# Two mixers of a hybrid trunk with another order of their TensorE groups, and two thirds of the second router's logits moved ahead

## What is computed

```python
def run_trunk(x, ...):
    for layer in range(2):
        h = rmsnorm(x, norm_mix[layer])
        if layer == 0:
            out = ab_mixer(h, ...)    # 4 heads mLSTM (matrix memory) and 4 heads retention with rotary q, k
        else:
            out = gdn_mixer(h, ...)   # 8 heads gated delta rule after a short convolution
        x = x + out
        x = x + hier_moe(rmsnorm(x, norm_ffn[layer]), ...)   # top group of 4, top 2 of its 8 experts
    return rmsnorm(x, norm_final)

def gdn_step(S, q, k, v, beta, g):   # one chunk; eg = exp(cumsum(g)), gam = decay between positions
    A = tril(beta * (k @ k.T) * gam, -1) + I
    u = solve(A, v * beta);  w = solve(A, k * (beta * eg))
    v_new = u - w @ S
    o = (q * eg) @ S + ((q @ k.T) * gam) @ v_new
    S = exp(g_last) * S + (k * exp(g_last - cumsum(g))).T @ v_new
```

## Time and profile before

| | |
|---|---|
| median of three runs | 1463.34 us (1462.14 to 1463.89) |
| profiled execution | 1466.4 us, of it the span 1464.6 us |
| mean granted TensorE clock | 0.909 |
| TensorE busy | 1153.2 us, 79% of the span |
| VectorE, ScalarE, GpSimd busy | 471.8, 250.5, 65.4 us |
| read from and written to HBM | 449.55 and 3.35 MB, 309 GB/s over the span |
| chain that ended last | PE 51%, DMA 38%, DVE 6%, issue 2% |

### The profile page before, as it was taken

How to read it: one execution, slowest core, us unless ns; L and a number is a source line. 1 busy time by engine, 2 the same in 40 slices (tenths; PEclk the granted TensorE clock), 3 DMA queues, 4 the chain that set the end, 5 groups by cost and what they waited for, 6 DMA issues and landing times.

```text
span 1464.6 us, 27531 instructions
## 1 busy us (share of the span) xinstructions
PE 1153.2 (79%) x11710; PEld 717.3 (49%) x11710; DVE 471.8 (32%) x1211; ACT 250.5 (17%) x633; POOL 65.4 (4%) x100
## 2 busy tenths in 40 slices
PE   8999889878585776775899989888867768767675
PEld 6645546444252443442478666556534434434342
DVE  1023445432232221322343746345222213222133
ACT  2123214110010100100232414131100101010011
POOL 2001102100000000000200101001000000000001
PEclk9999899998998887889899999999998879898888
DMA  9843235999999999999833303139999999999994
GB/s 274 184 92 112 77 122 224 420 411 428 427 429 429 429 428 430 426 429 430 258 120 115 117 4 130 60 118 380 424 428 427 428 428 429 428 430 428 428 428 190
DMA packets 54146, 453.87 MB, mean 310 GB/s; under 512 B 5680, under 2 KB 6480, under 8 KB 29760
## 3 DMA queue, kind: packets, MB, share of 16 engines
q1 hardware_dynamic: 52176, 448.35, 75.8%
q0 software_dynamic: 1904, 4.58, 1.2%
HBM read 449.55 MB, written 3.35 MB: 309 GB/s over the span
## 4 chain that ended last, share of the span: by engine, by line
PE 51%; DMA 38%; DVE 6%; issue 2%; ACT 1%; SPq 1%; POOL 1%; DVEq 0%; ACTq 0%; POOLq 0%
PE bank L341 49%; DMA W<-in_moe_w_up 37%; PE bank L344 1%; DMA W<-in_ab_w_in 1%; SPq L2484 1%; DVE zT L2332 1%; DVE HN L1593 0%; DVE HN L1573 0%; ACT zT L1538 0%; DVE gain L1573 0%; DVE HT L1573 0%; DVE zT L2337 0%; DVE X L1573 0%; DVE TM L1573 0%; DVE zT L1573 0%
## 5 line engine op out<-in xcount | busy, mean ns | idle before, releaser
L341 PE MATMUL bank<-W,zT 128*32 128x256 f32 (+1 forms) x6272 | 509.0, 454 | 171.1 <-DMA W<-in_moe_w_up 144.5
L341 PEld LDWEIGHTS bank<-W,zT 128*32 128x32 f32 (+1 forms) x6272 | 251.0, 127 | 386.6 <-issue 267.5
L2332 DVE TENSOR_TENSOR zT<-zT,bank 64x256 f32<-64x256 f32 x64 | 27.0, 422 | 408.1 <-ACT zT L1538 408.0
L341 PE MATMUL bank<-W,HT 128*32 128x128 f32 (+1 forms) x768 | 135.2, 398 | 3.3 <-ACT TM L1273 2.3
L341 PE MATMUL bank<-HT,W 128*128 128x288 f32 x512 | 126.9, 408 | 1.5 <-DMA W<-in_ab_w_in 1.5
L341 PEld LDWEIGHTS bank<-HT,W 128*128 128x128 f32 x512 | 96.6, 190 | 28.1 <-DMA W<-in_ab_w_in 2.0
L2342 DVE COPY zT<-bank 32x256 f32<-32x256 f32 x128 | 53.3, 416 | 156.8 <-PE bank L341 154.8
L341 PEld LDWEIGHTS bank<-zT,HN 128*128 128x128 f32 (+1 forms) x832 | 98.6, 195 | 9.7 <-issue 8.3
L341 PE MATMUL bank<-zT,HN 128*128 128x128 f32 (+1 forms) x832 | 101.5, 282 | 1.0 <-DVE HN L1573 0.7
L341 PE MATMUL bank<-const,zT 64*128 64x64 f32 (+3 forms) x340 | 47.6, 289 | 68.6 <-DVE zT L2332 68.2
L1544 ACT COPY zT<-bank 32x256 f32<-32x256 f32 x128 | 46.6, 364 | 264.2 <-PE bank L341 262.6
(11 more groups left out here) (285 smaller groups left out, 881.9 us busy)
## 6 DMA issues: line engine op xcount, KB each, us to landing
W<-in_moe_w_gate SPq DMA_DIRECT2D x62, 2048.0 KB, 18.0
W<-in_moe_w_up SPq DMA_DIRECT2D x62, 2048.0 KB, 22.5
W<-in_moe_w_down SPq DMA_DIRECT2D x62, 2048.0 KB, 22.4
W<-in_ab_w_in SPq DMA_DIRECT2D x8, 2048.0 KB, 16.5
W<-in_c_w_in SPq DMA_DIRECT2D x8, 2048.0 KB, 14.0
W<-in_ab_w_out SPq DMA_DIRECT2D x2, 2048.0 KB, 7.8
TM<-in_moe_w_gate SPq DMA_DIRECT2D x2, 2048.0 KB, 19.4
zT<-in_moe_w_up SPq DMA_DIRECT2D x2, 2048.0 KB, 15.3
```

What stands on the lines that cost most here:

```text
L341: return nc.tensor.matmul(out, lhsT, rhs, start=start, stop=stop)
L2332: v.tensor_tensor(hid[u % 2], sg[u % 2], banks[2 + u % 2][64:128, 0:2 * P], ALU.mult).then_inc(m["hidden"], 1)
```

## The change

**First mixer.** The second half of unit (6, 1) is split into two quarters that go into the second and third place of tile 2; unit (7, 0) takes the fourth place, ahead of tile 2's `finish_half`, and its place between the loops is empty. ScalarE takes (6, 1) before it copies tile 2's transposed scores, and still takes (7, 0) after the first loop. VectorE rotates tile 0 within tile 2 of the first loop, right after `diag`, with a scratch of its own (`early_half`).

**Second mixer, tile 1.** The products of `half` that don't need the inverse (k times state, scores, q times state, the transposes) move into the four block levels in place of output parts; the values are scaled by beta when they are copied, and the state's part is added to them in level 0 (`read_scale`). The eight output parts move to the places before and after pairs, halves, values and outputs. Norms, flips and the final product are reordered: `finish_half` of both halves stands before the product, tile 0's `flip_x` and the logits of tiles 2 and 0 between its two halves. The product goes to banks 4 and 5. `add_output(0)` comes after both norms. GpSimd's norm of tile 0 moves behind `state_done`, ahead of the store of the state. After the product `experts(1)` has one tile of logits left.

```diff
-          [[(6, 2, _ALL), (6, 1, _LOW)], [], [], [(6, 1, _HIGH)]]]
+          [[(6, 2, _ALL), (6, 1, _LOW)], [(6, 1, (4, 5))], [(6, 1, (6, 7))], [(7, 0, _ALL)]]]
...
 # TensorE, layer_ab, second loop
-                    else:
-                        project_tokens([(7, 0, _ALL)])
...
 # TensorE, layer_c, tile 1
-                for lv in range(3):
-                    output_part(0, 2 * lv)
-                    block_level_y(1)
-                    output_part(0, 2 * lv + 1)
-                    block_level_t(1)
-                block_level_y(1)
-                output_part(0, 6)
-                block_level_t(1)
+                E["state_ready"].wait(pe)
+                for lv in range(4):
+                    for f in range(2):
+                        if lv == 0:
+                            state_products(f, 8)
+                        elif lv == 1:
+                            first_scores(f, 1)
+                        elif lv == 2:
+                            state_products(f, 0)
+                            first_scores_T(f)
+                        (block_level_t if f else block_level_y)(1)
+                output_part(0, 0)
                 pairs_y()
                 E["u_ready"].wait(pe)
-                output_part(0, 7)
+                output_part(0, 1)
                 pairs_t()
+                output_part(0, 2)
                 halves_y()
+                output_part(0, 3)
                 halves_t()
+                output_part(0, 4)
                 for f in range(2):
                     E["tu_ready"].wait(pe)
-                E["state_ready"].wait(pe)
-                c = COL[1]
+                first_values()
+                output_part(0, 5)
                 for f in range(2):
-                    half(1, f, ..., delta=True)
+                    first_outputs(f)
+                output_part(0, 6)
+                output_part(0, 7)
                 finish_half(1, 0)
                 flip_x(2)
-                flip_x(0)
-                E["yT_act"].wait(pe)
-                E["out_taken"].wait(pe)
-                side.emptied(pe)
-                for p in range(2):
-                    output_half(1, p, range(4))
                 finish_half(1, 1)
...
                 E["yT_act"].wait(pe)
                 for p in range(2):
+                    output_half(1, p, range(4))
+                flip_x(0)
+                E["router_w"].wait(pe)
+                E["out_taken"].wait(pe)
+                router_logits(2)
+                router_logits(0)
+                E["yT_act"].wait(pe)
+                for p in range(2):
                     E["out_ready"].mark(output_half(1, p, range(4, 8)))
...
 # TensorE, experts(1)
                     flip_x(1)
-                    router_logits(2)
-                    router_logits(0)
                     router_logits(1)
...
 # ScalarE, layer_c
-                    if t:
-                        do(nc.scalar.copy(TM[:n, 20:24, :], heads4(bank[:n, :])), L1.taken)
-                    else:
-                        for h in range(4):
-                            do(... scale=beta[:, 4 + h:5 + h] ...)
+                    for h in range(4):
+                        do(... scale=beta[:, 8 * t + 4 + h:8 * t + 5 + h] ...)
...
 # VectorE, layer_ab
                     diag(a3[:n, t, :], n)
+                    if t == 2:
+                        rotate(0, early_half)
...
 # VectorE, layer_c
                     for lv in range(4):
+                        if t:
+                            second_tile(lv, 0)
                         bank = L0.take(dve)
                         tt(Y, blocks_of(bank), bc_mid(merges_s[:, lv], w), ALU.mult, L0.taken)
                         signal(E["yi_ready"])
...
+                        else:
+                            second_tile(lv, 1)
                         bank = L0.take(dve)
                         tt(T, T, blocks_of(bank), ALU.subtract, L0.taken)
...
+            def second_tile(lv, f):
+                col = lambda w: c_out[:, 1, w + 4 * f:w + 4 * f + 4]
+                if lv == 3:
+                    tt(first_kw[f], TM[:, 8 + 4 * f:12 + 4 * f, :], bc_last(col(8), P), ALU.mult, E["kw_ready"])
+                    return
+                bank = L0.take(dve)
+                if lv == 0:
+                    v_ = TM[:, 16 + 4 * f:20 + 4 * f, :]
+                    by_head(v_, heads4(bank[:, :]), read_scale[:, 4 * f:4 * f + 4], v_, ALU.mult, ALU.add, L0.taken)
+                    if f:
+                        signal(E["r_ready"])
+                elif lv == 1:
+                    tt(first_S[f], heads4(bank[:, :]), GAM[f], ALU.mult, L0.taken)
+                    signal(E["s_ready"])
+                else:
+                    tt(Yout[:, 4 * f:4 * f + 4, :], heads4(bank[:, :]), bc_last(col(0), P), ALU.mult, L0.taken)
...
                     signal(E["state_done"])
                     if t:
-                        E["gates_ready"].wait(dve)
-                        head_norm(t, (1,), (0, 4), 0, (2, 0))
+                        for f in range(2):
+                            normed(f)
+                            if not f:
+                                take_x(2)
+                        add_output(0)
+                        take_x(0)
+                        clear_logits()
+                        take_logits(2)
+                        take_logits(0)
...
 # GpSimd
                             norm_tile(2)
-                            norm_tile(0)
...
                         E["state_done"].wait(pool)
...
+                        else:
+                            norm_tile(0)
                     store(a["out_gdn"][0].rearrange("h k v -> k h v"), states[1])
```

More of the change, by code:

```diff
@@ L1438, in layer_c @@
                     bank = L1.take(act)
[L1439 to L1444 removed]
+                    for h in range(4):
+                        do(nc.scalar.activation(TM[:, 20 + h, :], bank[:, h * P:h * P + P], ACT.Copy,
+                                                scale=beta[:, 8 * t + 4 + h:8 * t + 5 + h]), L1.taken if h == 3 else None)
                     E["tm_act"].mark(act.nop())
```

131 lines of the change are left out of this document (76 added, 55 removed).

## The result

The changed kernel takes 1460.58 us (median of 12 runs, 1453.31 to 1464.84); the kernel before, beside it, takes 1467.49 (12 runs, 1459.81 to 1477.88). The ratio is 0.9947, 95% interval 0.9926 to 0.9968: faster by 7.8 us, between 4.7 and 10.9. The forecast was 1453.1. The kernel before is itself slower than its first three runs showed: over all 114 runs made in this study its median is 1468.05, not 1463.34. Of the 7.5 us by which the forecast is too low, 4.2 are this base (1467.49 beside it, the first three runs among its twelve) and 3.3 are the change, which is -6.9 by the two medians and was forecast at -10.2. A second comparison gave 0.9947 again (0.9922 to 0.9973). Three executions in a far slower state, one of the kernel before (1542.13) and two of `first_filled` (1673.07 and 2810.80), are in none of the ratios.

A forecast was written before the change was run, and what follows sets the result against it. Paths to the mixer's end (layer 0) and expert 0 (layer 1), which start the expert-matrix streams, bound the kernel; -7.6 - 4.7 + 2.1 = -10.2 from 1466.4 gives 1456.2, 3.1 lower on the runs' median: 1453.1; range 1449.5 to 1458.5.

The forecast's parts named there:

- b): First mixer, tile 2: no sparse TensorE stretch left, so full clock expected; -3.0 us, bounds -1.5 and -3.5.
- a): First mixer, tile 2: the 5.65 us of unit (6, 1) goes into TensorE's waits, ending about 0.3 late; -5.65 + 0.3.
- d): First mixer: VectorE's 5.47 us rotation moves into its 5.52 us wait before tile 2's maximum; nothing on the path.
- e): First mixer: ScalarE's table load and Silu for (7, 0) delay the copy to `ab_k`; +0.5 us, or +1.9 with a drain.
- The levels: Second mixer's four block levels: 16.9 us walked, start 0.5 later, ending about 935.9, so the pairs start 1.9 us earlier.
- Rival B: Block levels don't shorten: each of eight small-product groups pays 0.74 us idle by issue, +5.2; total 1458.3; chance 0.15.
- Rival D: Clock falls in block level 0, returning only with output parts 0 and 1; +3.3 us in all, 1466.6; chance 0.04.
- From pairs to flips: Second mixer, pairs to tile 1's flips: 47.9 us becomes 47.1, 42.9 busy and 4.2 idle; flips 2.6 earlier at 984.5.
- f): Second mixer, between output part 7 and the final product: one clock fall, +2.1 us; bounds 0 and 4.2.
- The logits: Behind tile 1's flips one router product is left of three: 5.5 us becomes 3.4, -2.1.
- C: First mixer's gain is swallowed by layer 0's matrix stream: -2.6 us in all, 1460.7, no measurable change; chance 0.07.
- A: No fall of the clock at f): -12.3 us in all, 1451.0; chance 0.22.

The follow-up runs named there:

- `first_filled`: Kernel before with only the change's first-mixer part, plus many products without a use in the first mixer's TensorE waits; 1459.03 us, ratio 0.9904 against the kernel before.
- `logits_back`: Changed kernel with the router products of tiles 2 and 0 returned behind tile 1's transposes; 1458.57 us, ratio 0.9933 against the kernel before.
- `rotate_back`: Changed kernel with the rotation of tile 0 back at the head of the second loop; 1467.48 us, ratio 0.9973 against the kernel before.

## Why the prediction was right and wrong

**The base.** The last step of the sum, "the median of the runs is 3.1 lower, 1463.34, so the forecast is 1453.1", failed most. It took three runs to stand for the kernel's middle. The profiled execution of before (1466.4) stood nearer to it (median 1468.05, 1459.8 to 1482.4 but for one run); of all 114 runs only 22 are as short as the longest of the three. Why these three were short, no run says. Taken from the profile without the shift, the forecast is 1456.2, from the median over all runs 1457.9, and with the base measured beside the change (1467.49) it is 1457.3, with a range that would reach to 1462.7 and hold the 1460.58. The other 3.3 are a change smaller than its sum, -6.9 to -7.8 for -10.2; by the traces that is b), a low stretch of the clock counted as gone for good, and the loop behind it.

**First mixer.** a) and d) held: the units fill the waits, the rotation is hidden. The sum up to the rotated transposes was -8.1 (the -7.6 without the 0.5 behind them), and the trace at full clock has 31.9 - 23.4 = -8.5. e) was right in kind: the copy to `ab_k` is late by 1.49 - 0.83 = 0.66, where 0.5 stood. The Silu starts 0.01 after the table load; the drain of about 1380 ns that the Trainium skill, "ScalarE: Activation LUTs", section "What ACT_TABLE_LOAD costs", adds to a switch isn't in this trace either, and keeping 0.5 was right. b) was the mis-sized term: -3.0 was taken for a low stretch gone for good. With the new order thirteen traces read 23.4 to 26.7 up to the rotated transposes, 25.2 in the mean, so 1.8 of the 3.0 came back at (7, 0). And the loop behind it, which the prediction called "the same", has a spread of its own, 62.1 to 71.8, which blurs what arrives: the first part by itself measured -5.1 for -7.6, with an interval that holds both.

**Second mixer.** The total came out near the forecast (the traces say about -4, the run of this part -5.1, forecast -2.6 with the clock term) by errors that cancel. The levels took +2.1 instead of -1.9 (and the 22.5 of before is itself long: other traces of its order read 21.0 to 22.0). The walk through their steps came out near: `logits_back`, whose clock stays up there, has levels of 21.9 with 1.95 of stalls in them, so 19.9 without, for the prediction's 20.6. (The 935.9 at which it lets the levels end does not follow from the rows it names; 919.32, 0.5 and 16.9 make 936.7.) What it put at nothing is the wait for instructions and the clock. Rival B was half of it: the idle time by issue doesn't strike every group, but in level 0 it lasts 0.85 to 1.73, since the read of an expert's matrix holds up TensorE's instructions. The prediction noted the 0.74 and the read's DMA share, but not that they stand at the same time; the 0.74, too, ends 1.2 after a packet of the instruction queue. Rival D's mechanism was the other half: a fall in level 1 (twice 2.08 - 1.16, and 0.33 for each of two small groups, 2.5) and one at the levels' end (0.33 and 3.12 - 1.98, 1.5), instead of one that lasts through all levels. The Trainium skill, "Runtime: NRT & Kernel Launch", section "Instruction fetch mechanics", says that the sequencer fetches its instructions by a DMA queue of its own, with refills mostly hidden. The traces agree with the first, as every stall follows a packet of the instruction queue; with the second they don't here, as 0.85 to 2.07 beside or right behind a 2 MB read is not hidden. From pairs to flips the forecast was -0.7 before the clock term, measured -3.7: I let 1.5 of the half-clock excess of the earlier trace rows go, and the whole of it, 3.3, went; and of 4.2 idle 3.1 were left. f) did not come in the changed kernel (7.03 and 7.11 for the final product), but did in five traces of kernels made from it (8.5 to 8.7), so it is a chance and not a term. The logits: -2.1 behind the flips was -0.7. At full clock it would have been -1.5 (3.7, as in `rotate_back`), as the lone product takes 1.95 and not 1.5; the rest is the clock, which falls at it (2.74 for 1.95). The 2.9 ahead of the flips was paid in full, as forecast.

**Rivals.** C fell: layer 0's stream keeps its length (482.7 after, 483.3 before; in the mean 483.5 in thirteen traces with the first part and 483.8 in four without it). That its 1460.7 is the time measured is chance: it is reckoned from the low base, with a change of -2.6. A was right in its mechanism, no fall at f), and not in its time. B and D were each partly right, about different places in the levels.

## What to carry to other kernels

A profile is one draw where TensorE's stretches are sparse: before a low-clock stretch is put into a sum as a cost that goes away, look whether the new order is dense, and take the spread from several traces or runs of the same code, the base's too. An order by which TensorE's wide products leave the small steps they covered can pay twice, in idle time and in clock. Here a couple of wide products kept there, products without a use in the first mixer's waits and two logits put back gave about 10 us beyond the change, all together. A stall by issue inside a run of short products is worth holding against the packets of the instruction queue, and against a large read beside it or just before. Work moved ahead of a wait is free only where the trace shows the engine idle there.

## What was unexpected in the hardware

TensorE can stand still for want of instructions inside straight-line products: here in dense runs of 32x32 products, at places 127 matmul records apart, for up to 0.93 us with no read near, and for up to 2.07 us beside or right behind a 2 MB read (DMA share 0.77 to 1.01), when the packet of instructions started late. Moved, the read took the long stall with it. The same code's second loop of the first mixer took 64.4 and 71.8 us in two executions, by the clock alone, and idle products of some 7 us in all made it repeat within 0.1 in every trace with the same order and filling.
